# Gates, branches and half of the queries with the weights stationary and the tokens moving, in a two-layer hybrid diffusion step

## The reference, cut to what matters

```python
h = rmsnorm(x, g_attn) * (1 + scale1) + shift1
zf, zq, zk, zv, zp = jnp.split(h @ w_in, IN_SPLITS, axis=-1)
# attn: 8 heads of neighbourhood and dense attention from zq, zk, zv
branch_f = fourier_mix(zf) @ w_fourier        # 256 -> 1024
branch_a = attn @ w_attn                      # 512 -> 1024
branch_p = pool_mix(zp, w_pool_grp, pool_scale) @ w_pool   # 256 -> 1024
gf, ga, gp = jnp.split(jax.nn.sigmoid(h @ w_gate + b_gate), 3, axis=-1)
x = x + gate1 * ((gf * branch_f + ga * branch_a + gp * branch_p) @ w_out)
h2 = rmsnorm(x, g_ffn) * (1 + scale2) + shift2
q = (h2 @ peer_wq).reshape(B, L, PEER_HEADS, 2, PEER_D_KEY // 2)   # 1024 -> 2048
s = jnp.einsum('blhpc,hpnc->blhpn', q, peer_keys)
# top 16 of the sums of two keys choose experts; their up and down projections, dense over 128 x 128
```

## Time and profile before

| what | value |
|---|---|
| time, median of 3 runs | 3347.4 us (3346.68 to 3349.25) |
| the profiled execution's own time | 3345.03 us |
| its span, first to last instruction | 3342.9 us |
| mean granted TensorE clock | 0.978 |
| PE busy | 3187.6 us, 95% of the span |
| PEld busy | 2777.9 us, 83% |
| DVE busy | 2068.4 us, 62% |
| ACT, POOL busy | 1014.1 us and 1012.0 us, 30% each |

### The profile page before, as it was taken

The page is one execution under the profiler, slowest core; times in us unless marked ns, Lnnn a source line. Parts: engine busy times, 40 slices in busy tenths (PEclk is TensorE's granted clock), DMA queues, the critical chain, the costliest instruction groups (busy, mean ns, idle before and its releaser), DMA issues.

```text
span 3342.9 us, 47511 instructions
## 1 busy us (share of the span) xinstructions
PE 3187.6 (95%) x16594; PEld 2777.9 (83%) x16594; DVE 2068.4 (62%) x4132; ACT 1014.1 (30%) x1348; POOL 1012.0 (30%) x434
## 2 busy tenths in 40 slices
PE   7898988999999999999989987999999999999998
PEld 4576767999999988888867766799999999888887
DVE  3145459900898467777753555598079965777775
ACT  2122233333344332222222322243344433222222
POOL 3233344644444410000015334356544442000000
PEclk8999989999999999999989998999999999999999
DMA  8822224674666666565643223244456667565653
GB/s 324 277 84 95 101 101 154 248 266 179 220 208 208 231 249 235 205 246 210 235 141 130 95 82 109 93 147 173 173 193 208 208 198 284 220 238 203 247 211 123
DMA packets 252643, 631.09 MB, mean 189 GB/s; under 512 B 25920, under 2 KB 130304, under 8 KB 231552
## 3 DMA queue, kind: packets, MB, share of 16 engines
q1 hardware_dynamic: 241440, 623.98, 52.7%
q10 hardware_dynamic: 11104, 5.81, 0.6%
HBM read 526.43 MB, written 107.06 MB: 190 GB/s over the span
## 4 chain that ended last, share of the span: by engine, by line
issue 76%; POOL 23%; POOLq 1%; DMA 0%; ACTq 0%; DVE 0%; ACT 0%
POOL wlo L600 22%; DMA x<-in_x_sample 0%; POOLq L599 0%; POOL rstd L596 0%; POOLq L612 0%; POOLq L595 0%; POOLq L604 0%; POOLq L142 0%; ACTq L634 0%; DVE x L1668 0%; ACT u L646 0%; ACTq L635 0%; POOLq L608 0%; ACTq L648 0%; POOLq L593 0%
## 5 line engine op out<-in xcount | busy, mean ns | idle before, releaser
L600 POOL TENSOR_TENSOR wlo<-raw,whi 128x1024 fp32r<-128x1024 f32 x400 | 996.7, 2495 | 1207.1 <-ACT whi L767 633.9
L1138 PE MATMUL acc<-lt_hi,whi 128*128 128x384 f32 x2048 | 698.1, 341 | 17.2 <-POOL wlo L600 13.4
L1138 PE MATMUL acc<-lt_lo,whi 128*128 128x384 f32 x2048 | 687.8, 336 | 0.0
L1138 PE MATMUL acc<-lt_hi,wlo 128*128 128x384 f32 x2048 | 687.2, 336 | 0.0
L1164 PE MATMUL acc<-whi,bt_lo 128*128 128x512 f32 x1488 | 578.9, 389 | 0.0
L1164 PE MATMUL acc<-wlo,bt_hi 128*128 128x512 f32 x1488 | 578.9, 389 | 0.0
L1164 PE MATMUL acc<-whi,bt_hi 128*128 128x512 f32 x1488 | 578.8, 389 | 0.0
L776 ACT ACTIVATE whi<-raw 128x1024 fp32r<-128x1024 f32 x256 | 271.6, 1061 | 749.4 <-PE acc L1164 748.0
L1632 DVE TENSOR_TENSOR wlo<-raw,whi 128x1024 fp32r<-128x1024 f32 x256 | 316.7, 1237 | 242.5 <-ACT whi L776 242.4
L1609 DVE TENSOR_SCALAR u<-iota,u 128x128 f32<-128x128 f32 x768 | 398.0, 579 | 42.9 <-issue 31.7
L1138 PEld LDWEIGHTS acc<-lt_hi,whi 128*128 128x128 f32 x2048 | 386.7, 189 | 28.1 <-issue 24.5
(11 more groups left out here) (174 smaller groups left out, 3486.8 us busy)
## 6 DMA issues: line engine op xcount, KB each, us to landing
raw<-in_ut SPq DMA_DIRECT2D x128, 1024.0 KB, 4.9
raw<-in_peer_v SPq DMA_DIRECT2D x128, 1024.0 KB, 4.8
acts<-u SPq DMA_DIRECT2D x128, 384.0 KB, 2.3
gmat<-u SPq DMA_DIRECT2D x48, 1024.0 KB, 5.1
z<-gmat SPq DMA_DIRECT2D x32, 1536.0 KB, 7.8
u<-acts SPq DMA_DIRECT2D x32, 1536.0 KB, 8.2
tables<-in_w_ada SPq DMA_DIRECT2D x15, 2048.0 KB, 9.4
raw<-in_w_gate SPq DMA_DIRECT2D x24, 1024.0 KB, 5.1
```

Of the source, the lines that this page charges most:

```text
L600: pool.tensor_tensor(wlo[:, slot], raw[:, slot], whi[:, slot].bitcast(F32), ALU.subtract).then_inc(lo_ready, 1)
L1138: mm = pe.matmul(acc[j][:, 0:T], w[:, j, c * P:(c + 1) * P], x[:, c, :], start=(c == 0 and q == 0), stop=(c == KC - 1 and q == 2))
```

## The change

The three gates, the three branches and the second half of the queries are computed transposed: 128 output columns of a weight are stationary and the 384 tokens move, so the result has channels on the partitions. A unit there holds 256 input channels x 512 output columns; `block_unit` does 4 blocks x 2 channel chunks x 3 parts = 24 matmuls of 384 columns, into four banks, so a pass has two halves of four banks each. The bias of a gate is then one number per partition: ACT takes the sigmoid straight from PSUM with it, right after each half; the DMAs of `GTB` and DVE's `gate` are gone. `merge` runs after each half of a branch pass, one chunk of 128 channels at a time; for the last branch it also casts and subtracts, so that the chunks are ready for w_out, and the 8 transposes of `M` with their copies are gone. The second half of the queries goes from PSUM to `PQT` by ACT (`asked`); its copies to `Z` and 8 transposes are gone. Banks are now counted through both layers, with one counter for those that ACT reads and one for those that DVE reads (`emptied`).

The other change of the call: the masked bias is added between the two "y" steps; the next layer's column loads stand behind the first four expert units on ACT; ACT's casts of the first four expert units stand between its copies of queries and scores; and SP loads all four pairs of GF ahead of the tables.

```diff
+                def blocks(u0, u1, w, n0, depth):
+                    v = w[l].rearrange("(k p) n -> p k n", p=P)
+                    for i, u in enumerate(range(u0, u1, 2)):
+                        sp.wait_ge(lo_ready, l * LOS + u + 2)
...
+                            sp.dma_start(slots.rearrange("p s (k n) -> p (s k) n", k=2),
+                                         v[:, k:k + 4, n0 + c * HB:n0 + (c + 1) * HB]).then_inc(pair_landed[u // 2 % 2], 16)
...
-                    pairs(U_GF, U_GF + 4, rows(a["w_gate"], 0))
+                    blocks(U_GF, U_WF, a["w_gate"], 0, KC)
                     sp.wait_ge(early_used, 8)
...
+                def sigmoid(o, c):
+                    act.wait_ge(cols_landed, l * (16 * 8) + 16 * 8)
+                    if o:
+                        act.wait_ge(gt_used, l * (3 * KC) + (o - 1) * KC + 4 * c + 4)
+                    for k in range(4 * c, 4 * c + 4):
+                        use = (C_GF, C_GP, C_GA)[o] + k
+                        act.wait_ge(acc_done, l * ACCS + use + 1)
+                        act.activation(GTB[:, k], accum(l, use)[:, 0:T], ACT.Sigmoid, bias=bgate[:, (0, 2, 1)[o], k:k + 1])\
+                           .then_inc(acc_read, 1)
...
-                queries(1, X_QB, 0, 8)
-                for t in range(TB):
-                    scores(1, X_SB, t)
...
+                hi(U_PEER)
+                asked(1)
+                act.drain().then_inc(pqt_ready, 1)
+                hi(U_PEER + 1)
+                scores(1, X_SB, 0)
+                hi(U_PEER + 2)
+                scores(1, X_SB, 1)
+                scores(1, X_SB, 2)
+                hi(U_PEER + 3)
...
+                def block_unit(u, lt, k0, use, first, last, beside=None):
+                    pe.wait_ge(lo_ready, l * LOS + u + 1 + SLOTS)
+                    s = u % SLOTS
+                    for b in range(4):
+                        if beside and b == 2:
+                            beside()
+                        if first:
+                            emptied(use + b)
+                        for e in range(2):
+                            lh, ll = (x[:, k0 + e, :] for x in lt)
+                            at = slice(e * HB + b * P, e * HB + (b + 1) * P)
+                            for n, (w, x) in enumerate(((whi, lh), (whi, ll), (wlo, lh))):
+                                mm = pe.matmul(accum(l, use + b)[:, 0:T], w[:, s, at], x,
+                                               start=first and e == 0 and n == 0, stop=last and e == 1 and n == 2)
+                        if last:
+                            mm.then_inc(acc_done, 1)
+                    (pe.drain() if last else mm).then_inc(unit_used, 1)
...
-                turned_pass(M, X_MT, lambda k: pe.wait_ge(m_ready, l * 2 + k // 4 + 1) if k % 4 == 0 else None,
-                            U_OUT, C_OUT, KC)
+                for k in range(KC - SLOTS):
+                    pe.wait_ge(ht_ready, l * (3 * KC) + KC + k + 1)
+                    unit(U_OUT + k, (LTh, LTl), k, C_OUT, k == 0, False)
+                by_tile(U_OUT + KC - SLOTS, (LTh, LTl), KC - SLOTS, C_OUT)
...
+                    if (kind, i) == ("y", 1):
+                        masked_bias()
...
+                def merge(o, c):
+                    if o == c == 0:
                         dve.wait_ge(kv_stored, l * 32 + 32)
+                    for i in range(4 + (0, 1, 3)[o]):
+                        k = 4 * c + i
+                        if i < 4:
+                            use = (C_WF, C_WP, C_WA)[o] + k
+                            dve.wait_ge(acc_read, l * READS["act"] + o * KC + k + 1)
+                            g, b = (x.rearrange("p (t n) -> p t n", t=TB) for x in (GTB[:, k], accu(use)[:, 0:T]))
+                            dve.tensor_tensor(g if o else M[:, k], g, b, ALU.mult).then_inc(acc_free, 1)
+                        if o and 1 <= i <= 4:
+                            dve.tensor_tensor(M[:, k - 1], M[:, k - 1], GTB[:, k - 1].rearrange("p (t n) -> p t n", t=TB), ALU.add)
+                        if o == 2 and 2 <= i <= 5:
+                            dve.tensor_copy(LTh[:, k - 2].rearrange("p (t n) -> p t n", t=TB), M[:, k - 2])
+                        if o == 2 and i >= 3:
+                            h, x = (y[:, k - 3].rearrange("p (t n) -> p t n", t=TB) for y in (LTh, LTl))
+                            dve.tensor_tensor(x, M[:, k - 3], h.bitcast(F32), ALU.subtract)
                         x = dve.drain()
+                        if o == 2 and i >= 3:
+                            x.then_inc(ht_ready, 1)
```

More of the change, by code:

```diff
@@ L72, with read_number @@
 C_GF = C_IN + 12
-C_WF = C_GF + 6
-C_GP = C_WF + 6
-C_WP = C_GP + 6
-C_GA = C_WP + 6
-C_WA = C_GA + 6
-C_OUT = C_WA + 6
+C_WF = C_GF + KC
+C_GP = C_WF + KC
+C_WP = C_GP + KC
+C_GA = C_WP + KC
+C_WA = C_GA + KC
+C_OUT = C_WA + KC
 C_Q = C_OUT + 6
-C_V = C_Q + 12
+C_QT = C_Q + 6
+C_V = C_QT + KC
 ACCS = C_V + 6 - C_IN
-FREES = ACCS
-assert ACCS % 6 == 0
+READER = ["dve"] * 12 + (["act"] * KC + ["dve"] * KC) * 3 + ["dve"] * 12 + ["act"] * KC + ["dve"] * 6
+assert len(READER) == ACCS
+READS = {who: READER.count(who) for who in ("dve", "act")}
+def read_number(n):
+    l, use = divmod(n, ACCS)
+    at = use
+    for c in (C_OUT, C_V):
+        if c <= use < c + 6:
+            h, t = divmod(use - c, TB)
+            at = c + 2 * t + h
+    who = READER[use]
+    return who, l * READS[who] + READER[:at].count(who) + 1
 STEPS = HEADS * TB
@@ L259, in build @@
         acc_free = sem("acc_free")
+        acc_read = sem("acc_read")
+        gt_used = sem("gt_used")
         aux_done = sem("aux_done")
@@ L455, in layer @@
                 pairs(U_Q + 4, U_Q + 8, lambda i: wq[:, i + 2, :, 0:UW])
-                pairs(U_Q + 8, U_PEER, rows(a["peer_wq"], UW))
+                blocks(U_Q + KC, U_PEER, a["peer_wq"], UW, KC)
                 def u_load(p, half):
@@ L711, in layer @@
                             exps(j)
-                    if u in (U_WF, U_WP, U_WA):
-                        sigmoid((U_WF, U_WP, U_WA).index(u))
+                    for o, u0 in enumerate((U_GF, U_GP, U_GA)):
+                        if u in (u0 + 3, u0 + 7):
+                            sigmoid(o, (u - u0) // 4)
                 for u in range(U_OUT + 2, U_Q + KC + 2):
@@ L744, in layer @@
                         scores(0, X_SA, k - 3)
-                queries(1, X_QB, 0, 8)
-                for t in range(TB):
-                    scores(1, X_SB, t)
-                if not last:
-                    act.wait_ge(pq_ready, l * 2 + 1)
-                    columns(l + 1)
-                for u in range(U_PEER, U_PEER + SLOTS):
-                    hi(u)
+                    if k == 3:
+                        asked(0)
+                hi(U_PEER)
[7 more added lines that the diff above has]
+                hi(U_PEER + 3)
                 def gelu(i, j, first):
@@ L809, in layer @@
                 if not last:
+                    columns(l + 1)
                     for p in range(6):
@@ L940, in turned_pass @@
                 def turned_pass(src, base, ready, u0, use, ht0):
-                    late = KC - SLOTS if u0 == U_OUT else KC
                     for k in range(KC + 3):
@@ L1116, in layer @@
                             score(X_SA, 0, 2 * (k - 3) + n)
-                    unit(U_Q + KC + k, (LTh, LTl), k, C_Q + 6, k == 0, k == KC - 1)
-                pe.wait_ge(pq_ready, l * 2 + 2)
-                for k in range(8, 16):
-                    query(X_QB, k)
+                    block_unit(U_Q + KC + k, (LTh, LTl), 2 * (k % 4), C_QT + 4 * (k // 4), k % 4 == 0, k % 4 == 3)
                 pe.wait_ge(pqt_ready, l * 2 + 2)
@@ L1425, in probabilities @@
                     dve.tensor_scalar(PR[:, s, 0:n], PR[:, s, 0:n], rsum[:, s:s + 1], None, ALU.mult).then_inc(pn_ready, 1)
-                def gate(n, use):
-                    dve.wait_ge(bgate_landed, l * 48 + 16 * (n + 1))
-                    for h in range(2):
-                        for t in range(TB):
-                            g = GTB[:, t, h * HB:(h + 1) * HB]
-                            dve.tensor_tensor(g, g, accu(use + TB * h + t)[:], ALU.add).then_inc(acc_free, 1)
-                        dve.drain().then_inc(gate_sum, 1)
@@ L1463, in layer @@
                         dve.drain().then_inc(att_done, 1)
-                    for u1, what, n, use in ((U_WF, gate, 0, C_GF), (U_GP, merge, 0, C_WF), (U_WP, gate, 1, C_GP),
-                                             (U_GA, merge, 1, C_WP), (U_WA, gate, 2, C_GA), (U_OUT, merge, 2, C_WA)):
-                        if u + 1 == u1:
-                            what(n, use)
-                columns(X_MT, MRAW, lambda k, b: dve.tensor_copy(MRAW[:, k], b[:, 0:T]))
+                    for o, (u0, u1) in enumerate(((U_WF, U_GP), (U_WP, U_GA), (U_WA, U_OUT))):
+                        per = (u1 - u0) // 2
+                        if u0 <= u < u1 and (u - u0) % per == per - 1:
+                            merge(o, (u - u0) // per)
```

(2 more changed lines are left out.)

129 lines of the change are left out of this document (57 added, 72 removed).

## The result

| what | before | after |
|---|---|---|
| time, median of 4 runs each, on one chip | 3348.3 us (3346.7 to 3353.1) | 3288.9 us (3286.6 to 3293.8) |
| ratio, 95% interval | | 0.9822 [0.9805, 0.9839] |
| the profiled execution's own time | 3345.0 us | 3289.3 us |
| its span | 3342.9 us | 3287.5 us |
| mean granted TensorE clock | 0.978 | 0.986 |

The forecast was 3303, the range 3280 to 3324: the time is in the range and 14 under the forecast, and it lies outside the forecast's own narrower range, 3291 to 3316. Between the two spans lie 55.4 us. PE's busy time falls by only 22.0 of them; the rest is waiting that went.

What follows compares the result with a forecast made beforehand. PE, busy 95% of the span, bounds the kernel, so only fewer or cheaper matmuls or less waiting help. Terms 12.8 - 6 + 5 + 20 + 24 - 11 = 45 off 3347.4 gave 3303 us, range 3280 to 3324.

Steps and rivals of the forecast that it cites:

- (a): Layer 0 gate-stage start: moving the bias ends PE's 12.8 wait and a slow start; new table wait of 2; +12.8.
- (b): Masked bias at "y", 4.43 on DVE, delays WF's start and WF0's third bank: -3 per layer, -6 in all.
- (c): Branches WF and WP: DVE some 2 late per half instead of 5, but twice; half of 7 per layer back: +5.
- (d): WA to w_out: transposes, copies and waits go, at most 13.8 per layer; late banks lose 4: +20 in all.
- (e): Last query unit to first expert unit: 20.2 and 16.0 become about 7.0, plus about 2 for slow starts: +24.
- (f): New transposed units: 0.08 more on each of 80 units, -6.4, and 14 more drains, -4.9; together -11.
- starved weights: Rival: w_gate loads in 2 KB runs land too late for PE; 3450 if a pair takes 12; chance 0.04.
- no gain: Rival: PE's waits come back as waits for ACT, stopped at each half; about 3345; chance 0.04.
- The port does not bite: Rival: DVE's small sums and casts slip between POOL's subtractions; 20 more saved, 3283; chance 0.24.
- DVE becomes the bound: Rival, branches: each sum and cast is held, score copies and w_out's banks come late; 30 less saved, 3333; chance 0.22.

Runs made afterwards that it cites:

- the run without them: Changed kernel with the four products of WA's second half put ahead of the first half's second and third differences; 3279.6 us, ratio 0.9803.

## Why the prediction was right, step by step

(a) *Start of the gate stage*: 12.8 predicted, 14.5 measured (the saving of layer 0 without that of layer 1, 14.00 + 0.51). The wait and its slow start went as said. The new wait of 2 for the tables did not come: they landed at 160.4, not 166.5. I had added 5 for the pair of weights ahead of them in the queue, and that did not show: issued within 2.5 us, pair and tables each landed 5 to 8 us after its own issue.

(b) *Bias at "y"*: -3 a layer predicted, -2.5 measured, by the run with the bias one step earlier. The two places of the wait were right, but a third was missing: POOL's delayed subtractions came in a burst later and held DVE beside WF1, and PE waited 1.45 at "v".

(c) *Branches*: +5 predicted. From the first z to WA0, without (a), the table gives -1.5 in layer 0 and -3.1 in layer 1, -4.6. Of that the bias is -5.0 and the price of the new units and drains (below) -7.2, so the branches are left with +7.6. That is what remains by subtraction, with a price that was measured on the query units alone. It is near +5 by luck, since it does not stand where I put it. I had expected half of the 7 per layer at WP back; from WP0 to GA0 both layers got longer, by 1.38 and 1.45, of which 0.43 is the price. The 7.6 are +2.9 from WF0 to GP0, +6.6 in the three gate passes and -2.0 at WP, and no run here shows what made the gate passes shorter. The waits at WP's "v" were 3.78 and 1.65 (distances of the matmuls around them), where 1 to 3 were said. The step that failed is the sums: I had priced product and sum at 0.47 and 0.44 and put no figure on POOL. Unheld they took 0.55 each and held up to 2.02; their place cost 4.8 to 5.3 a layer, net, of which POOL's hold was 2.6 to 2.7.

(d) *WA to w_out*: +20 predicted; 9.58 and 7.89 measured, and 1.5 of price for the new units in it: 19.0. Layer 1 would have had 1.65 more without its stretch at 0.79. The waits for banks lost 3.1 in layer 0, by the run without them (2.2 idle of PE), where 4 was said. The mechanism, products behind sums, casts and differences, is shown by the run in which they vanish.

(e) *End of the queries*: +24 predicted; 21.9 for the way to the experts and 4.5 for the slow start that went, 26.4. Of it the place of the casts and column loads in ACT's list carries 16.1, by the stages of the run with the casts last. The slow starts were 2.05 and 2.44, where 2 was said for both together. The way took 7.21 and 7.93, where 7.0 was said.

(f) *Price of the new units*: -11 predicted. The matmuls of the new units stand 0.173 apart, as said. Eight query units, with one more drain among them, take 0.91 more: 8 x 0.08 + 0.27. By that, as an estimate, a layer pays 4 x 0.91 for the three gates and the query half, 0.43 each for WF and WP and 0.75 for WA, where a drain without a step beside it showed as 0.43: 5.25, so -10.5. The estimate of 1.3 for the units by the Trainium skill ("TensorE: Matmul & The Clock Gate", section "Back-to-back issue gap") would have been far under their 6.4.

The sum in the profile is 14.5 - 5.0 + 7.6 + 19.0 + 26.4 - 10.5 = 52.0, and 3.4 in places that I had not listed (the table's stage up to the query's ninth unit, the start and the stretch between the layers) make 55.4. The sum fell short by 7: in (a) by a wait that did not come, in (c), and in (e) by counting one slow start for two. The medians differ by 3.6 more than the profiled times, since the profiled execution of before stood 3.3 under its median and that of after 0.3 over.

Of the rivals, starved weights and no gain are ruled out by the rows above. The time, 3288.9, lies nearer to that of "The port does not bite" (3283) than to the forecast, but the rival is false as said: the port bites at the sums, the cast at "y" and the differences, and (b), (c) and (d) came to -5.0, 7.6 and 19.0 where it had 0, 12 and 27. "DVE becomes the bound" holds for WP alone.

## What to carry to other kernels

Cut the timeline of the bounding engine into stages and compare them one by one: a net loss of 1.4 in a stage (WP0 to GA0) hid a loss of 6.7 that a new order of the sums took out of it, and such a loss is the next edit. When a result is assembled from small elementwise steps, put those that free a bank ahead of those that only prepare the next operand. Let one input of a sum stay in PSUM, or move the sum to where nobody waits, when GpSimd is at work on SBUF at the same time.

## What the runs showed of the hardware

The cast of a chunk from `M`, three runs of 128 numbers per partition, took 0.54 to 0.55 in all 16 cases, and one ran wholly inside a POOL subtraction (356.37, POOL from 356.24 to 358.72), while the contiguous cast at "y" took 0.36 alone (197.11) and 2.45 when POOL ran. The form of the cast that is slower alone was the faster one beside POOL. The difference of the same chunk, with both inputs in SBUF, took up to 2.61 (second row; minimum/median/maximum in ns):

```profile
L1503 DVE CAST lt_hi<-z x16: 539/546/554, 356.4 to 2003.9; 128x384 fp32r<-128x384 f32 x16
```

```profile
L1506 DVE TENSOR_TENSOR lt_lo<-z,lt_hi x16: 543/554/2611, 359.5 to 2005.0; 128x384 fp32r<-128x384 f32 x16
```

The same waits were followed by a lower clock in some stages and not in others. Three of 0.7 to 0.8 idle in w_out's first unit were followed by a mean granted clock of 1.00 in layer 0 and of 0.79 in layer 1, from the same instructions. Of the twelve w_out stages with these three waits, in the profiles of six kernels, three had such a stretch, two of them in layer 0, and took 37.24 to 37.30 instead of 35.65 to 35.76. The stretches behind the waits in the changed kernel (us, busy us and instructions of PE PEld DVE ACT POOL, PEclk, DMA):

```profile
1998.80:2006.80 8.00, 8.00 (x28) 6.42 (x29) 6.43 (x9) 2.12 (x2) 2.46 (x2) 0.79 0.25 102
...
370.60:378.60 8.00, 8.00 (x35) 6.61 (x36) 6.41 (x9) 2.13 (x2) 4.16 (x2) 1.00 0.18 73
```

In layer 1 28 matmuls of 512 columns fit into the 8 us, in layer 0 35.
